# Token mixer of a two-block transformer on one core: softmax loop, state-space products and gate stores in another order

## The reference, cut to what matters

```python
def token_mixer(h, ...):
    proj = h @ w_in                        # 512 x 1024 by 1024 x 4104
    u, q, k, v, f, g_a, g_b = split(proj)  # g_a, g_b: 512 x 1024 each
    y_ssm = s5_ssm(u, ...)                 # 32 groups, 64 complex states
    z_val, z_gate = split(gelu(y_ssm) @ glu_w)
    y_a = z_val * sigmoid(z_gate)
    attn = forgetting_attention(q, k, v, f + forget_b)  # 8 heads, causal
    y_b = attn @ attn_w_out
    merged = sigmoid(g_a) * y_a + sigmoid(g_b) * y_b
    return merged @ w_out
```

## Time and profile before

| | |
|---|---|
| median of 3 runs | 3547.41 us (3530.92 to 3552.03) |
| the profiled execution, its own time | 3543.86 us |
| its span, first to last instruction | 3542.1 us |
| mean granted TensorE clock | 0.956 |
| busy share: PE, PEld, DVE, ACT, POOL | 95%, 74%, 57%, 33%, 38% |
| mixer, first pass: gate block 9 ends, first attention step begins | about 1647 us |
| mixer, second pass: the same place | about 2874 us |

### The profile page before, as it was taken

How to read it: one execution, slowest core, us unless ns; L and a number is a source line. 1 busy time by engine, 2 the same in 40 slices (tenths; PEclk the granted TensorE clock), 3 DMA queues, 4 the chain that set the end, 5 groups by cost and what they waited for, 6 DMA issues and landing times. The chain is left out here.

```text
span 3542.1 us, 44586 instructions
## 1 busy us (share of the span) xinstructions
PE 3349.0 (95%) x16330; PEld 2617.3 (74%) x16330; DVE 2012.5 (57%) x2706; ACT 1172.8 (33%) x1792; POOL 1340.4 (38%) x565
## 2 busy tenths in 40 slices
PE   8999999999997999899999999889998999989997
PEld 6657787657775888787776888668887876778886
DVE  3876685876775445995374442244459944654412
ACT  3354323355323223332334222232233324332232
POOL 3302343302333445452152445434464421534453
PEclk9999999999997999998899999989999988999999
DMA  4524472524453332486142332143235941423321
GB/s 131 167 75 125 126 229 86 158 72 128 137 173 94 96 91 87 82 123 97 48 121 61 107 95 84 53 110 97 85 90 86 123 80 54 129 76 95 92 84 62
DMA packets 587985, 363.85 MB, mean 103 GB/s; under 512 B 58146, under 2 KB 537772, under 8 KB 587564
## 3 DMA queue, kind: packets, MB, share of 16 engines
q1 hardware_dynamic: 587444, 361.51, 39.5%
q10 hardware_dynamic: 376, 0.12, 0.0%
HBM read 346.63 MB, written 12.58 MB: 101 GB/s over the span
## 5 line engine op out<-in xcount | busy, mean ns | idle before, releaser
L152 POOL TENSOR_TENSOR w_lo<-w_raw,w_hi 128x1024 fp32r<-128x1024 f32 (+2 forms) x552 | 1332.4, 2419 | 2154.1 <-ACT w_hi L144 2154.1
L158 PE MATMUL bank<-xh,w_lo 128*128 128x512 f32 x2432 | 983.5, 404 | 45.6 <-DVE xl L2365 26.1
L160 PE MATMUL bank<-xh,w_hi 128*128 128x512 f32 x2432 | 968.3, 398 | 0.0
L159 PE MATMUL bank<-xl,w_hi 128*128 128x512 f32 x2432 | 967.6, 398 | 0.0
L144 ACT ACTIVATE w_hi<-w_raw 128x1024 fp32r<-128x1024 f32 (+2 forms) x552 | 565.5, 1028 | 797.2 <-PE bank L160 723.2
L158 PEld LDWEIGHTS bank<-xh,w_lo 128*128 128x128 f32 x2432 | 466.3, 192 | 168.6 <-issue 42.6
L159 PEld LDWEIGHTS bank<-xl,w_hi 128*128 128x128 f32 x2432 | 467.2, 192 | 104.8 <-issue 4.3
L160 PEld LDWEIGHTS bank<-xh,w_hi 128*128 128x128 f32 x2432 | 466.4, 192 | 103.0
L158 PE MATMUL bank<-HH,w_lo 128*128 128x512 f32 x704 | 278.6, 396 | 0.0
L160 PE MATMUL bank<-HH,w_hi 128*128 128x512 f32 x704 | 278.5, 396 | 0.0
L159 PE MATMUL bank<-HL,w_hi 128*128 128x512 f32 x704 | 278.4, 395 | 0.0
(11 more groups left out here) (507 smaller groups left out, 4541.5 us busy)
## 6 DMA issues: line engine op xcount, KB each, us to landing
w_raw<-in_ffn_w_in_dram SPq DMA_DIRECT2D x176, 512.0 KB, 3.8
m_raw_l<-in_mod_w_dram SPq DMA_DIRECT2D x128, 512.0 KB, 5.0
w_raw<-in_w_in_dram SPq DMA_DIRECT2D x80, 512.0 KB, 4.0
w_raw<-in_mix_w_in_dram SPq DMA_DIRECT2D x64, 512.0 KB, 9.4
w_raw<-in_ffn_w_out_dram SPq DMA_DIRECT2D x64, 384.0 KB, 3.4
w_raw<-in_ffn_w_out_dram SPq DMA_DIRECT2D x64, 320.0 KB, 3.1
m_half_l<-in_mod_w_dram SPq DMA_DIRECT2D x32, 256.0 KB, 2.7
w_raw<-in_w_out_dram SPq DMA_DIRECT2D x16, 512.0 KB, 5.0
```

The costliest lines, as they stand in the source:

```text
L152: nc.gpsimd.tensor_tensor(ring.lo[s][:, 0:width], ring.raw[s][:, 0:width], ring.hi[s][:, 0:width].bitcast(F32), ALU.subtract).then_inc(rin ...
L158: nc.tensor.matmul(out, wl, xh, start=start, stop=False)
L159: nc.tensor.matmul(out, wh, xl, start=False, stop=False)
L160: return nc.tensor.matmul(out, wh, xh, start=False, stop=stop)
```

## The change

Five things are done together.

- **Memory.** `PTr` moves from `Kn` to the second half of `Btr` (the states' work tiles `sa` and `sb` lie there, done with by then). `Yc`, the gelu tile `gt` and `zl` move to `Kn`. ScalarE's wait for `m_in` is taken out; TensorE's own wait for it before state-space product 0 stays. ScalarE now waits for `states` before the first `exps` instead of before gate 7.
- **Staging.** Only the two `stg` tiles are used, so the exponentials no longer wait for stores from `sqt`. Blocks 8 and 9 use PSUM banks 6 and 7.
- **Last gate.** Gate block 9 comes after `scores(0)` and `scores(1)` on TensorE, and after `exps(0)` to `exps(3)` on ScalarE.
- **State-space products.** They stand in steps 2 to 5 instead of 0 to 3 (`YS = 2`). The gelu starts two iterations j later, that is one step.
- **Stores.** ScalarE issues the store of gates 0 to 11 itself, right after the tanh and the weight split; SyncE issues none.

The core of the diff:

```diff
+    Kn = mem("Kn", [P, CH, P], F32)
     Btr, Bti = mem("Btr", [P, GP, P], F32), mem("Bti", [P, GP, P], F32)
...
-    Zr, Zi, Xr = (mem(x, [P, GP, NC], F32, over="Btr", skip=(1 + i) * half) for i, x in enumerate(("Zr", "Zi", "Xr")))
-    Yc = mem("Yc", [P, NG, NC], F32, over="Btr")
+    Zr, Zi, Xr = (mem(x, [P, GP, NC], F32, over="Btr", skip=i * half) for i, x in ((0, "Zr"), (2, "Zi"), (3, "Xr")))
+    Yc = mem("Yc", [P, NG, NC], F32, over="Kn")
...
-    PTr = [mem(f"PT2{i}", [P, TT, P], F32, over="Kn", skip=i * 16 * P) for i in range(2)]
+    PTr = [mem(f"PT2{i}", [P, TT, P], F32, over="Btr", skip=half + i * 16 * P) for i in range(2)]
...
-        hold(("g", f), f % 4)
+        hold(("g", f), f % 4 if f < NFA - 2 else f - NFA + 8)
...
-    staged = [0, 0, 0, 0, 0, 1, 0, 2, 3, 1, 0, 1]
+    staged = [0, 0, 0, 0, 0, 1, 0, 1, 0, 1, 0, 1]
...
-        def gate_out(f):
-            wait_read(sp, ("g", f))
-            sp.dma_start(g_dram[f], buffer(f)[:, :]).then_inc(kept(f)[0], 16)
...
-        for f in range(3, NFA):
+        for f in range(3, NFA - 1):
             gate(f)
...
         scores(0)
         scores(1)
+        gate(NFA - 1)
         for g in range(NS):
             turn_probs(2 * g)
-            if g < 4:
+            if g < YS + 4:
                 scores(g + 2)
             turn_probs(2 * g + 1)
-            if 4 <= g < NS - 2:
+            if YS + 4 <= g < NS - 2:
                 scores(g + 2)
-            if g < 4:
-                y_product(g)
+            if YS <= g < YS + 4:
+                y_product(g - YS)
...
             hi(B_G + 4 + f)
+            if f < 12:
+                wait_read(act, ("g", f))
+                act.dma_start(g_dram[f], dst[:, :]).then_inc(kept(f)[0], 16)
...
-            t, what = divmod(j - 18, 2)
+            t, what = divmod(j - 20, 2)
...
-            if j in (2, 3):
-                act.wait_ge(*kept(10 - j))
...
+        act.wait_ge(s["states"], 4)
         for j in range(4):
             exps(j)
-        act.wait_ge(s["m_in"], 16 * 32)
+        gate(NFA - 1)
...
-            t, what = divmod(j - 19, 2)
+            t, what = divmod(j - 21, 2)
```

More of the change, by code:

```diff
@@ L1454, in second_block @@
     Er, Ei = (mem(x, [P, GP, NC], F32, over="th0", skip=i * half) for i, x in enumerate(("Er", "Ei")))
-    sa, sb = (mem(x, [P, GP // 2, NC], F32, over="Btr", skip=i * half // 2) for i, x in enumerate(("sa", "sb")))
-    Zr, Zi, Xr = (mem(x, [P, GP, NC], F32, over="Btr", skip=(1 + i) * half) for i, x in enumerate(("Zr", "Zi", "Xr")))
-    Yc = mem("Yc", [P, NG, NC], F32, over="Btr")
-    gt = mem("gt", [P, 4, T], F32, over="Btr")
+    sa, sb = (mem(x, [P, GP // 2, NC], F32, over="Btr", skip=half + i * half // 2) for i, x in enumerate(("sa", "sb")))
+    Zr, Zi, Xr = (mem(x, [P, GP, NC], F32, over="Btr", skip=i * half) for i, x in ((0, "Zr"), (2, "Zi"), (3, "Xr")))
+    Yc = mem("Yc", [P, NG, NC], F32, over="Kn")
+    gt = mem("gt", [P, 4, T], F32, over="Kn")
     ych = mem("ych", [P, 4, CH, NC], F32, over="Bti")
-    zh, zl = mem("zh", [P, 4, T], F32R, over="Bti"), mem("zl", [P, 4, T], F32R, over="Btr")
+    zh, zl = mem("zh", [P, 4, T], F32R, over="Bti"), mem("zl", [P, 4, T], F32R, over="Kn")
     gtv = gt[:, :, :].rearrange("p t (c s) -> p t s c", s=CH)
@@ L1479, in second_block @@
              "b_powers", "b_turned", "c_powers", "k_taps", "m_cleared", "m_in", "u_out", "u_in", "injected",
[L1480 removed]
+             "states", "chunk_out", "gate_out0", "gate_out1", "gate_in0", "gate_in1", "y_out", "y_in", "y_sum", "gelu_square", "gelu_arg", "gelu_tanh",
              "skip_added", "z_split", "f_split", "f_logits", "f_biased", "f_exp", "f_log", "cum_ready", "scores", "maxima",
@@ L1527, in second_block @@
     for f in range(2, NFA):
-        hold(("g", f), f % 4)
+        hold(("g", f), f % 4 if f < NFA - 2 else f - NFA + 8)
     NI = HF * TT
     NS = NI // 2
+    YS = 2
     for f in range(NFA, NF):
         hold(("g", f), 7)
-    for j in range(8):
+    for j in range(2 * YS + 8):
         hold(("t", j), 4)
@@ L1538, in second_block @@
         hold(("s", j), j % 4)
-        if j >= 8:
+        if j >= 2 * YS + 8:
             hold(("t", j), 4 + j % 2)
@@ L1553, in second_block @@
     hold("post2", 4)
-    staged = [0, 0, 0, 0, 0, 1, 0, 2, 3, 1, 0, 1]
+    staged = [0, 0, 0, 0, 0, 1, 0, 1, 0, 1, 0, 1]
     def buffer(f):
-        return (stg[0], stg[1], PX[3], PX[2])[staged[f]]
+        return stg[staged[f]]
     def kept(f):
@@ L1699, in taps @@
                     sp.dma_start(to, Kn[32 * a:32 * a + SG, :, t * SG:P]).then_inc(s["m_in"], 16)
-        for f in range(8):
+        for f in range(10):
             gate(f)
-        for f in range(2):
-            gate_out(f)
-            gate(8 + f)
         sp.wait_ge(s["m_cleared"], 1)
@@ L1709, in _ @@
             taps(2 * i, 2 * i + 1)
-            gate_out(2 + i)
             gate(10 + i)
-        for f in (6, 7):
-            gate_out(f)
-            gate(8 + f)
-        for f in (8, 9):
-            gate_out(f)
-            merge_block(f - 8)
-        gate_out(10)
-        merge_block(2)
+        for f in (14, 15):
+            gate(f)
+        for i in range(3):
+            merge_block(i)
         wait_read(sp, ("y", 3))
@@ L1725, in _ @@
         sp.dma_start(ych[:, :, :, :].rearrange("p t s c -> p t (s c)"), y_dram.rearrange("(t p) c -> p t c", p=P)).then_inc(s["y_in"], 16)
-        gate_out(11)
-        merge_block(3)
-        for i in range(4, 10):
+        for i in range(3, 10):
             merge_block(i)
-        for f in (7, 8, 10, 11):
+        for f in (10, 11):
             sp.wait_ge(*kept(f))
@@ L2209, in _ @@
             read(nc.scalar.activation(dst[:, i % 4 * 4:i % 4 * 4 + 4, :].rearrange("p g c -> p (g c)"), held(("bt", i)), ACT.Copy), ("bt", i))
-        for f in range(2, NFA):
+        for f in range(2, NFA - 1):
             gate(f)
@@ L2255, in _ @@
                         exps(i)
-                if g < 4:
-                    take_chunk(g)
+                if YS <= g < YS + 4:
+                    take_chunk(g - YS)
                 f, ks = parts[g]
```

4 lines of the change are left out of this document (removed).

## The result

The changed kernel takes 3520.14 us (median of 9 runs, 3510.43 to 3526.47) against 3547.41 us (9 runs beside them, 3530.92 to 3554.5). The ratio is 0.9927, 95% interval 0.9911 to 0.9943. The profiled execution took 3520.14 us with a span of 3518.4 us, against 3543.86 and 3542.1: 23.7 us of span less. By the medians it is 27.3 us less; what follows explains the profiled pair. Its mean granted clock is 0.959 against 0.956.

A forecast was written before the change was run, and what follows sets the result against it. TensorE, 95% busy, was taken as the bound, so only its idle or low-clock stretches in the mixer counted: 8 + 7 + 3 = 18 us off 3543.86 gave 3526 us, range 3509 to 3546 (the forecast's own 3516 to 3538).

The forecast's parts named there:

- Part A: TensorE's hole between gate 9 and state-space product 0: 8 us saved over both passes, ends 3 and 10.5.
- Part B: State-space product 0 starts from the high clock: 3.4 us saved per pass, 7 us together, ends 0 and 8.
- Part C: End of attention: last three VectorE gelu operations follow the last probabilities, saving 3 us, ends -3 and 5.
- the 2 us per pass left for the late `PT`: Attention entry: TensorE still waits for ScalarE's first `PT` copy, 2 us per pass, between 0.8 and 4.6.
- The other doubt: Attention entry: gate 9 needs the landing of gate 7's store, both using `stg[1]`; a second way to the same delay.
- the wait that I named: Gate work of step 14 starts 2.08 us late behind ScalarE's `gr`; sign of success: that wait under 2 us.
- The parts at nothing: Gate 9's order, ScalarE's store issues, SyncE without stores and the chain of y: each costed at nothing.
- The slack of y: Chain of y, from product 3 through the `ych` fetch to the first gelu: some 8 us of slack remain.
- 1, full DMA engines: Attention entry: DMA engines, not the queue, are full, so the hole stays; 8 us saved, 3536 us; 20%.
- 2, ScalarE held by its issues: Gates 3 to 9 and entry: store issues over 3.9 us delay ScalarE; slower, 3555 us; 9%.
- 3, the clock kept: State-space products begun at the high clock keep it; 44 us saved with parts A and C, 3500 us; 5%.
- 4, nothing gained: The hole is refilled by an unseen wait and all parts cancel; 3544 us; 4%.

The follow-up runs named there:

- products_0_to_3: The changed kernel with the state-space products back in steps 0 to 3, gelu still one step later; ratio to before 0.9948, stretch 368.8 us.
- m_in_only: The kernel before, with the change's memory map and ScalarE's wait for the taps taken out; ratio to before 0.9992.
- m_in_restored: The changed kernel with ScalarE's wait for the taps put back behind gate 9's tanh; one execution, 3520.49 us, not compared.
- changed_again: The changed kernel itself, no line altered, measured again on one chip beside others; ratio to before 0.9942, 3520.87 us.
- stage_only: The kernel before, with gates 7 and 8 staged in `stg` and the exponentials' wait gone, stores still on SyncE; ratio to before 1.000.
- gelu_early: The changed kernel with the gelu back in the iterations of before, one step earlier; ratio to before 0.9956, stretch 372.3 us.
- sync_stores: The changed kernel with all gate stores issued by SyncE at their old places between its loads; ratio to before 0.995, stretch 374.6 us.
- halves: The changed kernel with each state-space product cut in two, one half ahead of the gate work, one behind `attend`; ratio to before 0.9954.
- interleaved: The changed kernel with the gate work of steps 2 to 5 put between groups of the state-space products; ratio to before 0.997.
- spread_over_8: The changed kernel with one half product in each of steps 0 to 7 and the gelu two iterations later; ratio to before 0.9944.

## Why the prediction was right, step by step

The forecast was 3526 us, 18 us less. The median of the runs, which is also the profiled execution, came at 3520.14: 23.7 us less than the profiled execution before, 27.3 less than its median. The mechanisms of parts A and B held. The number is less good than it looks. The upper ends of the three parts add up to 10.5 + 8 + 5 = 23.5 us, that is 3520.4, so 3516 as the lower end of the forecast's own range does not follow from them, and the result lies where all three upper ends meet. Parts A and C came out above theirs. By parts:

| part | forecast, us | measured, us | from |
|---|---|---|---|
| A, hole at the entry | 8 | 12.2 | start of product 0, before against products_0_to_3 |
| B, the products' length | 7 | 6.2 | 83.1 - 76.9, all eight rows |
| C, end of attention | 3 | 5.5 | the rest, 23.9 - 12.2 - 6.2 |
| sum | 18 | 23.9 | the stretch |

**Part A** had the right cause. That the store of `sqt` ended last and the taps' wait cost nothing is shown from both sides, by m_in_only and m_in_restored. (The working first dates its 11.1 us from the start of gate 9's last product; they run from its end, 1647.18, as part A has it.) The mis-sized term is the 2 us per pass left for the late `PT`: 0.40 us is left in both passes (0.63 and 0.39 in changed_again), below even my lower end of 0.8. An issue on ScalarE took 0.33 us, where I had taken 0.6 from the rows of `vrow`, and the copy ended 2.15 us after gate 9's last product began. The other doubt, the landing of gate 7's store ahead of gate 9's tanh, did not arise: that tanh waited for TensorE alone. It is real, however, as soon as SyncE issues (stage_only: 2.80 us at this very tanh, 6.92 us at the one before).

**Part B** was right for product 0: 3.2 and 3.8 us shorter, 7 in all. What I had not seen is that the others move too. The clock falls at another place in each product, and in the second pass products 2 and 3 took 1.0 and 1.2 us more than before. Such shifts of a microsecond came with every edit, down to m_in_restored. That the sum of all eight came near 7 us is in part luck, since I had counted on product 0 alone.

**Part C** was right in sign and sits in the right place, and gelu_early supports its size: 6.8 us lost, 5.4 without the longer products. But the step of the working behind it is wrong: the wait that I named is not the one that went. The 2.08 us for `gr` at step 14 are still there, and the sign that I had set, under 2 us, did not come; those for `ol` and `th` (2.03 + 0.53 and 1.93 + 0.51 us) are gone, and one of 1.28 for `sqt` came, in the first pass only. That is 3.7 us of the 5.5. Most of the other 1.8 us is the clock behind the last wait of the first pass. In the kernel before it fell there:

```profile
...
1778.00:1782.00 4.00, 4.00 (x13) 2.83 (x13) 3.08 (x5) 1.01 (x3) 2.47 (x1) 0.61 0.00 0
...
```

That costs 4.00 x (1 - 0.61) = 1.6 us of work at the high level. The changed kernel's clock stays at 1.00 from 1764 to 1776. This part is luck rather than design: in changed_again it stays up too, but in m_in_restored, products_0_to_3 and gelu_early, and in the second pass of all of them, it falls behind the same wait of 2.08 us.

**The parts at nothing.** ScalarE waited 16.9 us for its stores in four places, and its tanhs of gates 5 to 8 still came every 5.5 us, so the cover held. The slack of y was 8.7 us where I had some 8.

**The rivals.** 1, full DMA engines: no wait took the hole's place, and it matters which engine issues and behind what, as sync_stores shows. A store's landing can take 11.5 us from either engine, so slow landings do exist here; a store that goes out at once has the time for it. 2, ScalarE held by its issues: the longest took 383 ns, where over 3.9 us were wanted; SyncE's reached 3646. 3, the clock kept: it fell inside product 0 with TensorE busy throughout. The Trainium skill, "TensorE: Matmul & The Clock Gate", section "HAM oscillation — how this bites in real kernels", has idle gaps as the cause of the low level; the row at 1664 to 1668, 4.00 us busy at 0.60, disagrees, and halves, interleaved and spread_over_8 show that how much of the low level comes with these products depends also on what stands between them. 4, nothing gained: no.

**What stays open.** Why each fall of the clock comes where it does, and so the last 1 us of any product's length. Which property of the state-space products goes with it: they are 64 columns wide, 32 of a product's 48 matmuls read 64 partitions instead of 128, and there are many in a row; no run took these apart. Whether spread_over_8 is really faster than the changed kernel: its trace says 0.7 to 4.4 us, the comparison says nothing. A version with its short halves and an end without the 3.65 us was tried once, and failed on VectorE. And one rival inside part A: before, gate 7's tanh stood 6.53 us (at 1638.81) behind the states `Zi`, a wait that the change moved as well and that no run restores by itself. Gate 8's tanh, whose store the exponentials waited for, stood only 1.36 us, for TensorE, so its weight should be small; but that is argued.

## What to carry to other kernels

Where several waits stand in a row on one engine, find the one that ends last, and change that one: the taps' wait was worth nothing alone and nothing when put back. A store that frees a buffer is best issued by the engine that fills it, when the other engine has long issues in front of it: with fewer buffers but the stores left between SyncE's transfers (stage_only) the wait only moved to another instruction. A long run of narrow matmuls can leave TensorE at the low level without any gap. Cutting the run up over more steps made its own rows shorter, but look at the clock of the work behind each piece, and at the whole kernel, before calling that a gain: here no gain over the changed kernel is shown.

## What of the hardware had not been expected

- A store of 256 KB issued by SyncE between its loads can hold SyncE for 3.65 us (4.43 in the kernel before), while ScalarE's issues of the same stores never took over 0.38 us, with the same landing times of up to 11.5 us.
- The granted clock falls from 1.00 to 0.50 with TensorE busy 4.00 of 4 us in state-space products, 64 columns wide. With groups of three 512-wide matmuls set into each product it was 0.50 for over 20 us in both passes, those matmuls included, yet 0.91 over another 24 us of the second pass in the same order.
- Half of such a product (24 instructions) took 3.7 us at the high level. Alternating with a step of other work, 12 of 16 halves ran there, and the fall mostly came behind them: 1.00 from 1671 to 1675 in a half, 0.57 from 1675 to 1679 in 512-wide gate products.
